# Hybrid decoder step on one core: the Gx tiles' tanh one tile later in the order, their first tap on ScalarE, past rows summed once, a sample's query fetched one turn ahead

## The reference

```
token_mixer(xn):
    z = xn @ w_in                      # one projection for all branches and gates
    qkv, _ = causal_dwconv(concat([g_q, g_k, g_v]), hist['gdn_conv'], w)   # width 4, 1536 channels
    q, k, v = split(silu(qkv)); q = l2norm(q); k = l2norm(k)
    o_b = gated delta rule over (q, k, v), in chunks; rmsnorm; times silu(g_z)
    ya, _ = causal_dwconv(a_c * a_h, hist['sconv'], w)                     # width 3, 512 channels
    yc, _ = causal_dwconv(c_v * sigmoid(c_g), hist['conf'], w)             # width 31, 512 channels
    o_d = forgetting attention; for a sample: over 2048 past tokens, 16 cached pages of 128
    x += (sum_i sigmoid(gate_i) * (o_i @ w_branch[i])) @ w_out
cross attention; then
    g, u = xn @ w_ffn_in;  x += (silu(causal_dwconv(g, hist['ffn'], w)) * u) @ w_ffn_out   # width 3, 2816 channels
```

## Time and profile before

| | us |
|---|---|
| median of 3 runs | 1837.2 |
| lowest, highest | 1836.98, 1845.5 |
| the profiled execution | 1836.28 |
| its span | 1834.5 |
| TensorE busy in it | 1545.2 (84%) |
| VectorE busy | 917.6 (50%) |
| GpSimd busy | 643.9 (35%) |
| ScalarE busy | 555.8 (30%) |

### The profile page before, as it was taken

How to read it: one execution, slowest core, us unless ns; L and a number is a source line. 1 busy time by engine, 2 the same in 40 slices (tenths; PEclk the granted TensorE clock), 3 DMA queues, 4 the chain that set the end, 5 groups by cost and what they waited for, 6 DMA issues and landing times. The chain is left out here.

```text
span 1834.5 us, 28395 instructions
## 1 busy us (share of the span) xinstructions
PE 1545.2 (84%) x11127; PEld 1426.6 (78%) x11127; DVE 917.6 (50%) x1353; ACT 555.8 (30%) x893; POOL 643.9 (35%) x354
## 2 busy tenths in 40 slices
PE   4996577789796978999888879889577999999996
PEld 3896577579796977877666659888476999999995
DVE  4169887998956743113222232264425566663122
ACT  3322441112214212254222223444214333333222
POOL 1266544555664712222111104310402344443440
PEclk8898787899898989999889879999867999999998
DMA  7145323433353416447433106432312233332331
GB/s 213 48 132 155 110 81 98 134 103 114 110 149 104 129 51 199 143 146 227 119 110 116 41 13 195 131 92 81 121 46 75 81 93 93 93 93 77 96 99 47
DMA packets 250997, 199.86 MB, mean 109 GB/s; under 512 B 11620, under 2 KB 208797, under 8 KB 250456
## 3 DMA queue, kind: packets, MB, share of 16 engines
q1 hardware_dynamic: 234149, 169.47, 31.7%
q10 hardware_dynamic: 15723, 23.86, 3.8%
q0 software_dynamic: 992, 4.72, 0.7%
HBM read 187.89 MB, written 10.81 MB: 108 GB/s over the span
## 5 line engine op out<-in xcount | busy, mean ns | idle before, releaser
L762 POOL TENSOR_TENSOR rawl<-raw,wh 128x1024 fp32r<-128x1024 f32 (+2 forms) x196 | 428.6, 2188 | 1040.4 <-ACT wh L1145 1038.8
L802 PE MATMUL pb<-xh,wh 128*128 128x260 f32 x2176 | 649.9, 299 | 48.7 <-DVE xl L1516 22.6
L802 PE MATMUL pb<-xl,wh 128*128 128x260 f32 x2176 | 633.7, 291 | 0.0
L802 PE MATMUL pb<-xh,rawl 128*128 128x260 f32 x2176 | 632.0, 290 | 0.0
L802 PEld LDWEIGHTS pb<-xh,wh 128*128 128x128 f32 x2176 | 430.7, 198 | 65.9 <-issue 39.2
L802 PEld LDWEIGHTS pb<-xl,wh 128*128 128x128 f32 x2176 | 430.5, 198 | 0.7
L802 PEld LDWEIGHTS pb<-xh,rawl 128*128 128x128 f32 x2176 | 429.9, 198 | 0.0
L1145 ACT ACTIVATE wh<-raw 128x1024 fp32r<-128x1024 f32 (+2 forms) x208 | 201.6, 969 | 551.1 <-PE pb L802 521.7
L802 PE MATMUL sd<-ar 128*128 128x128 f32 (+5 forms) x1584 | 280.9, 372 | 96.2 <-DVE ar L1516 37.2
L802 PEld LDWEIGHTS sd<-ar 128*128 128x128 f32 (+4 forms) x1584 | 200.2, 199 | 142.0 <-issue 80.8
L773 POOL TENSOR_TENSOR ar<-ar 128x512 f32<-128x512 f32 x128 | 187.5, 1465 | 86.3 <-DMA ar<-in_cache_fox_k 58.5
(11 more groups left out here) (168 smaller groups left out, 1739.6 us busy)
## 6 DMA issues: line engine op xcount, KB each, us to landing
raw<-in_w_in SPq DMA_DIRECT2D x80, 512.0 KB, 4.1
ar<-in_cache_fox_k SPq DMA_DIRECT2D x128, 256.0 KB, 2.7
ar<-in_cache_fox_v SPq DMA_DIRECT2D x128, 256.0 KB, 3.1
raw<-in_w_ffn_in SPq DMA_DIRECT2D x44, 512.0 KB, 3.7
raw<-in_w_branch SPq DMA_DIRECT2D x32, 256.0 KB, 3.2
raw<-in_w_ffn_out SPq DMA_DIRECT2D x16, 512.0 KB, 3.9
ar<-in_cache_mem_k ACTq DMA_DIRECT2D x1, 4096.0 KB, 19.5
raw<-in_w_out SPq DMA_DIRECT2D x8, 512.0 KB, 3.9
```

What stands on the lines that cost most here:

```text
L762: pool.tensor_tensor(rawl[:, p % RING, 0:kt, :], raw[:, p % RING, 0:kt, :], wh[:, p % (AHEAD + 1), 0:kt, :].bitcast(F32), SUB).then_inc(lo ...
L802: return pe.matmul(o, l, r, start=start, stop=stop, skip_group_check=True)
```

## The change

- In `timeline()`, `evac`: for a Gx tile behind a Gx tile the second step (`evac2`) of the tile before is emitted behind the first step of this one; the last Gx tile's own follows at once. The `l2` steps wait one piece more.
- In `timeline()`, `background`: a flag `turned`; where a page that is the first of a sample (not the very first) is due and the flag is down, the flag is raised and nothing is emitted in that call.
- GpSimd asks for a sample's query behind the last product of the sample before, and waits for it at the sample's first product.
- ScalarE writes the last tap's product of Gx and `fg` tiles straight from PSUM, between the copy of the last columns and that of the tile; VectorE's product goes. `ah` tiles keep theirs.
- The past rows of all tiles are multiplied by their weights and summed once, in the prologue (`pasts`, seven VectorE instructions); a tile adds the sum in one small instruction. The waits between the taps in `conv` change accordingly.

```diff
--- before.py
+++ after.py
@@ -164,7 +164,7 @@
 
 SIDE = ([("AFTER", "fq", 0)] + [("sm", n) for n in range(4)]
         + [("AFTER", "fq")] + [("fqr", n) for n in range(2)] + [("KSTART",)]
-        + [x for n in range(4) for x in (("AFTER", "gx", 2 * n + 1), ("l2", n))] + [("l2", 4)]
+        + [x for n in range(4) for x in (("AFTER", "gx", min(11, 2 * n + 2)), ("l2", n))] + [("l2", 4)]
         + [("AFTER", "gx")]
         + [("gs", n) for n in range(9)]
         + [("gdn", n, c) for c in range(2) for n in range(-1, 18)]
@@ -215,11 +215,16 @@
 def timeline():
 
     out, pos, step_n, tile, at_piece, bg = [], [0], [0], [0], [-1], {"tap": None, "k": None, "v": None}
+    turned = [False]
     size = {"tap": N_TAP, "k": N_PAGE, "v": len(V_EVENTS)}
 
     def background(kind, n):
         for _ in range(n):
             if bg[kind] is not None and bg[kind] < size[kind]:
+                if kind == "k" and bg[kind] % PAGES == 0 and bg[kind] > 0 and not turned[0] and n < 10:
+                    turned[0] = True
+                    return
+                turned[0] = False
                 out.append(V_EVENTS[bg[kind]] if kind == "v" else (kind, bg[kind]))
                 bg[kind] += 1
 
@@ -253,8 +258,12 @@
     def evac(upto_piece):
 
         while tile[0] < len(MT_LAST) and MT_LAST[tile[0]] <= upto_piece:
-            out.append(("evac", tile[0]))
-            out.append(("evac2", tile[0]))
+            m = tile[0]
+            out.append(("evac", m))
+            if MT_KIND[m] == "gx" and MT_KIND[m - 1] == "gx":
+                out.append(("evac2", m - 1))
+            if MT_KIND[m] != "gx" or MT_KIND[m + 1] != "gx":
+                out.append(("evac2", m))
             tile[0] += 1
 
     def through(mark):
@@ -634,6 +643,10 @@
             "ef": [(tail_ff, 4 * j, min(4, KF - 4 * j), 10, 2, out["ff_p"][0, 0, :, 512 * j:min(512 * (j + 1), FF)],
                     out["ff_s"][:, 0, FCW - 2, 512 * j:min(512 * (j + 1), FF)]) for j in range(6)]}
 
+        gh = cols[:, B_GS:B_GS + 4, 0:72].rearrange("p n (b r) -> p n b r", b=2)
+        sh = cols[:, B_SS, 0:64].rearrange("p (b r) -> p b r", b=NB)
+        fh = cols[:, B_FS:B_FS + 4, 0:88].rearrange("p n (b r) -> p n b r", b=2)
+
         def both(x):
 
             return x.rearrange("p (a b) -> p a b", a=2)
@@ -762,15 +775,21 @@
                 pool.tensor_tensor(rawl[:, p % RING, 0:kt, :], raw[:, p % RING, 0:kt, :],
                                    wh[:, p % (AHEAD + 1), 0:kt, :].bitcast(F32), SUB).then_inc(lo.sem, 1)
 
+            def query(b):
+
+                pool.dma_start(qb[:, :], qscr[b:b + 1, :].to_broadcast([P, 512])).then_inc(qb_in, 16)
+
             def product(i):
 
+                if i == 0:
+                    pool.wait_ge(qs_out, 16)
+                    query(0)
                 if i % PAGES == 0:
-                    if i == 0:
-                        pool.wait_ge(qs_out, 16)
-                    pool.dma_start(qb[:, :], qscr[i // PAGES:i // PAGES + 1, :].to_broadcast([P, 512])).then_inc(qb_in, 16)
                     pool.wait_ge(qb_in, 16 * (i // PAGES + 1))
                 pool.wait_ge(page_in[i % 4], 16 * (i // 4 + 1))
                 own(pool.tensor_tensor(kring[:, i % 4, :], kring[:, i % 4, :], qb[:, :], MUL), prod_done)
+                if i % PAGES == PAGES - 1 and i < N_PAGE - 1:
+                    query(i // PAGES + 1)
 
             for p in range(AHEAD):
                 split(p)
@@ -1190,6 +1209,9 @@
                     n_ = 11 if kind == "gx" else 10
                     act_c.by(act.activation((tail_gx if kind == "gx" else tail_ff)[:, idx, :],
                                             pb[:, m % 2, 1, TH - n_:TH], ACT.Copy))
+                    y, w = (gx_tile(idx), col(V_GW + 36 + idx)) if kind == "gx" else \
+                        (pairA[:, s, :], cols[:, B_FW, 2 * KF + idx:2 * KF + idx + 1])
+                    act_c.by(act.activation(both(y), x, ACT.Copy, scale=w))
                     fn(both(cb[:, s, 3:3 + T]), x, ACT.Copy, mt_act)
                 elif kind == "ac":
                     fn(both(pairA[:, s, :]), x, ACT.Copy, mt_act)
@@ -1527,20 +1549,22 @@
             def red(o, x, op, st=dve_c):
                 own(dve.tensor_reduce(o, x, AX, op), st)
 
-            def conv(x, y, width, wcol, hist, w_last, st):
-
-                ts(y, x[:, 3:3 + T], w_last)
+            def conv(x, y, width, wcol, past, st):
+
+                ys = y[:, SEQ:T] if len(past.shape) == 2 else y[:, SEQ:T].rearrange("p (n b) -> p n b", b=2)
                 for j in range(width - 1):
                     if j:
-                        dve.wait_ge(dve_c.sem, dve_c.n - 1)
-                    dve_c.by(dve.scalar_tensor_tensor(out=y[:, 0:SEQ], in0=x[:, 4 - width + j:4 - width + j + SEQ],
-                                                      scalar=wcol(j), in1=y[:, 0:SEQ], op0=MUL, op1=ADD))
-                    past = hist(j)
-                    ys = y[:, SEQ:T] if len(past.shape) == 2 else y[:, SEQ:T].rearrange("p (n b) -> p n b", b=2)
-                    if j:
-                        dve.wait_ge(dve_c.sem, dve_c.n - 1)
+                        dve.wait_ge(dve_c.sem, dve_c.n - (j == 1))
                     (st if j == width - 2 else dve_c).by(dve.scalar_tensor_tensor(
-                        out=ys, in0=past, scalar=wcol(j), in1=ys, op0=MUL, op1=ADD))
+                        out=y[:, 0:SEQ], in0=x[:, 4 - width + j:4 - width + j + SEQ], scalar=wcol(j), in1=y[:, 0:SEQ], op0=MUL, op1=ADD))
+                    if j == 0:
+                        dve_c.by(dve.tensor_tensor(ys, ys, past, ADD))
+
+            def pasts(h, w, width, n):
+
+                tt(h, h, w, MUL)
+                for j in range(1, width - 1):
+                    tt(h[..., 0:n], h[..., 0:n], h[..., j * n:(j + 1) * n], ADD)
 
             def evac(m, second):
                 p = MT_LAST[m]
@@ -1570,17 +1594,12 @@
                     stt(glu[:, idx, CFW - 1:CFW - 1 + T], pairB[:, s, :], 1.0, pairA[:, s, :], ADD, MUL)
                     cp(tail_cf[:, idx, :], glu[:, idx, SEQ:SEQ + 38], ev_all)
                 elif kind == "gx":
-                    gh = cols[:, B_GS:B_GS + 4, 0:72].rearrange("p n (b r) -> p n b r", b=2)
-
-                    def hist(j):
-                        return gh[:, :, :, j * 12 + idx]
-
-                    conv(cb[:, s, :], gx_tile(idx), GCW, lambda j: col(V_GW + 12 * j + idx), hist, col(V_GW + 36 + idx), ev_y)
+                    conv(cb[:, s, :], gx_tile(idx), GCW, lambda j: col(V_GW + 12 * j + idx), gh[:, :, :, idx], ev_y)
                 elif kind == "ah":
                     tt(both(cb[:, s, 3:3 + T]), both(pairA[:, s, :]), x, MUL, mt_dve)
                     cp(tail_sc[:, idx, :], cb[:, s, SEQ + 1:SEQ + 11])
-                    conv(cb[:, s, :], pairB[:, s, :], SCW, lambda j: col(V_SW + 4 * j + idx),
-                         lambda j: cols[:, B_SS, 0:64].rearrange("p (b r) -> p b r", b=NB)[:, :, 4 * j + idx], col(V_SW + 8 + idx), ev_all)
+                    ts(pairB[:, s, :], cb[:, s, 3:3 + T], col(V_SW + 8 + idx))
+                    conv(cb[:, s, :], pairB[:, s, :], SCW, lambda j: col(V_SW + 4 * j + idx), sh[:, :, idx], ev_all)
                 elif kind == "ab":
                     tt(both(tmp), both(pairB[:, s, :]), x, MUL, mt_dve)
                 elif kind.startswith("br"):
@@ -1599,12 +1618,7 @@
                     stt(both(xT[:, idx, :]), x, 0.5 if kind == "wo" else 1.0, both(xT[:, idx, :]), MUL, ADD, mt_dve)
                     cp(fl8[:, 0:1], fl8[:, 1:2], ev_all)
                 elif kind == "fg":
-                    fh = cols[:, B_FS:B_FS + 4, 0:88].rearrange("p n (b r) -> p n b r", b=2)
-
-                    def hist(j):
-                        return fh[:, :, :, j * KF + idx]
-                    conv(cb[:, s, :], pairA[:, s, :], FCW, lambda j: cols[:, B_FW, KF * j + idx:KF * j + idx + 1], hist,
-                         cols[:, B_FW, 2 * KF + idx:2 * KF + idx + 1], ev_y)
+                    conv(cb[:, s, :], pairA[:, s, :], FCW, lambda j: cols[:, B_FW, KF * j + idx:KF * j + idx + 1], fh[:, :, :, idx], ev_y)
                 elif kind == "fu":
                     tt(both(tmp), both(pairA[:, s, :]), x, MUL, mt_dve)
 
@@ -1936,6 +1950,9 @@
             red(own_head, ident.rearrange("p (j r) -> p r j", r=32)[:, 0:FH, :], ADD)
             dve.wait_ge(wsm_hi.sem, 1)
             tt(wsl[:, :, :], wsm[:, :, :], wsh[:, :, :].bitcast(F32), SUB, wsm_lo)
+            for x, w, width, n in ((gh, cols[:, B_VEC, V_GW:V_GW + 36], GCW, 12), (fh, cols[:, B_FW, 0:44], FCW, KF)):
+                pasts(x, w[:, None, None, :].to_broadcast([P, 4, 2, (width - 1) * n]), width, n)
+            pasts(sh, spread(cols[:, B_VEC, V_SW:V_SW + 8], NB, 1), SCW, 4)
             spl = [0]
             for e in TIMELINE:
                 if e[0] == "nsq" and e[1] in ADDED and e[2] > 0:
```

## The result

The changed kernel takes 1898.4 us (median of 4 runs, 1896.55 to 1906.49), the kernel before 1839.1 beside it (4 runs): a ratio of 1.0316, 95% interval 1.0289 to 1.0343. The forecast was 1871 us, the range 1842 to 1908. The profiled execution took 1899.5 us, its span is 1897.7.

The account below looks back on a forecast made before the run. VectorE was taken to bound the stretch before 517 us, and TensorE the feed-forward stage. From 1836.3 us, +119 for pages emitted together at piece 61, -80 path relief and -4 for queries gave 1871 us, range 1842 to 1908.

Parts of the forecast that it names:

- The heap: At piece 61, 74 pages emitted at once, 1.40 us each plus four sample starts of 3.9: +119 us, ends 114 and 142.
- The relief on VectorE: Before piece 45 (517 us), page sums, stretching, first taps and past rows together take 104 us off VectorE.
- (a): Before 517 us, 75 page sums at 0.66 us leave VectorE: 50 us.
- (b): Before 517 us, VectorE's two-input instructions stretch less without GpSimd's page products beside them: 31 us, ends 0 and 55.
- the two signs named ahead: Tap times before piece 45: near 0.75 us would show the relief right, still over 1 us would show it wrong.
- (c): Before 517 us, the first tap of 12 Gx tiles goes to ScalarE: 13 us off VectorE.
- (d): Before 517 us, past rows need 12 small instructions instead of 36, and 4 of the A tiles instead of 8: 10 us.
- From VectorE to the path: Before 517 us, TensorE's 97 us idle less 17 for norm turns and chunk starts: path gain 80, ends 50 and 115.
- half the relief: Rival: splits, not products, do the stretching and delta-rule steps are bound by their own chain; gain 45, 1910 us; chance 0.10.
- The two queries: Queries behind pages 96 and 112 find their cover in the new order: 4 us gained, ends 0 and 7.
- TensorE runs without a gap: Rival: between pieces 12 and 45 chains close, all 115 us comes back, heap at 1.34 us a page; 1832 us; chance 0.11.
- The flag works as its words say: Rival: pages keep their pace, each sample one turn later, no heap; some 45 us gained, 1791 us; chance 0.05.

Follow-up runs that it names:

- flag alone: The kernel before plus only the changed kernel's `turned` flag, with old convolution, tanh order and query fetch: 1914.8 us, ratio 1.0388.
- short sums: The kernel before with VectorE's sums of pages 16 to 90 taken over 8 of a head's 64 elements: 1832.2 us, ratio 0.9942.
- short products: The kernel before with GpSimd's products of pages 16 to 90 over 64 of 512 columns, sums whole: 1811.5 us, ratio 0.9834.
- convolution alone: The kernel before with only `conv`, `pasts` and ScalarE's first tap from the change: 1835.0 us, ratio 0.9963.
- order alone: The kernel before with only the new order (a Gx tile's tanh behind the next tile's first step, norms one piece later): 1836.7 us, ratio 0.9965.
- products on VectorE: The changed kernel without the flag, with products of pages 16 to 90 moved from GpSimd to VectorE, ahead of their sums: 1838.0 us, ratio 0.9987.
- products wait, 12 to 44: The changed kernel without the flag; in pieces 12 to 44 GpSimd's page products wait for VectorE's chain work of the turn: 1832.4 us, ratio 0.9958.
- without the flag: The changed kernel with its four flag lines taken out, so pages keep the old pace: 1827.2 us, ratio 0.9919.
- mended flag: The changed kernel, but only a page lowers the flag, not a tap, so pages are held one turn per sample: 1840.5 us, ratio 0.9987.
- products wait, 12 to 23: The changed kernel without the flag; in pieces 12 to 23 GpSimd's page products wait for VectorE's chain work of the turn: 1825.1 us, ratio 0.9919.
- taps and pages moved behind: The changed kernel without the flag, with 10 pages and 8 taps moved behind piece 44: 1833.5 us, ratio 0.9965.
- fewer pages, late: The changed kernel without the flag, one page per two turns up to piece 44, 7 per four behind, samples' steps later: 1816.6 us, ratio 0.9846.

## Why the prediction was right, and where it was mis-sized

The forecast had the direction and both large terms, and 1898 lies in its range. It is still 27 us above the 1871, because its terms erred to the same side: some 19 of it are the relief, 3 the heap, 3 the queries, and 2 came behind piece 62.

**The order** was right as read from the code: no page from piece 13 to 44, 74 pages in one heap.

**The heap** was right in place and price: 119 forecast, 122.2 measured; 1.40 and 3.9 forecast, 1.43 and 4.2 measured, and nothing covers it.

**The relief on VectorE** was 94.0 us (340.98 to 246.98), forecast 104. The pages' part, (a) and (b), was right as a sum: 81 forecast, 79.7 with the flag alone. How it splits was not shown by it, and short sums and short products show that the two terms do not add like this: what leaves VectorE changes what the rest falls beside. The taps came out between the two signs named ahead: 970 ns, neither near 750 nor over 1000. Convolution and past rows, (c) and (d), together with the new order brought 14.3 (261.25 to 246.98) instead of 23. The 9 are here, in VectorE's groups of the changed kernel and in order of time:

```profile
L1662 DVE SCALAR_TENSOR_TENSOR ar<-xT,cols,ar 128x512 f32<-128x512 f32 x112 | 103.3, 970 | 1.2
L1558 DVE SCALAR_TENSOR_TENSOR ar<-ar,cols 128x512 f32<-128x512 f32 x44 | 42.4, 962 | 18.7 <-ACT ar L1164 18.2
...
204.37 1.70 DVE L1558 SCALAR_TENSOR_TENSOR ar<-ar,cols 128x512 f32<-128x512 f32 x1 [4.13 <-ACT ar L1164]
...
203.12 2.40 POOL L775 TENSOR_TENSOR rawl<-raw,wh 128x1024 fp32r<-128x1024 f32 x1 [12.02 <-ACT wh L1164]
```

The 44 convolution taps take 962 ns; with the old convolution and no pages, 747: 9.5 us. A row of that kernel, the one with the flag alone, shows one way there. VectorE's first tap stood beside the split and waited for it:

```profile
203.43 2.01 DVE L1524 TENSOR_SCALAR ar<-ar,cols 128x520 f32<-128x520 f32 x1 [2.06 <-ACT ar L1150]
...
202.77 2.39 POOL L767 TENSOR_TENSOR rawl<-raw,wh 128x1024 fp32r<-128x1024 f32 x1 [11.36 <-ACT wh L1150]
```

Of its 2.01 us some 0.5 are its own work (0.49 where GpSimd does nothing beside it). In the changed kernel this instruction is gone and the next one has the wait: 1.70 us, to 206.07, behind the split's end at 203.12 + 2.40 = 205.52. I had priced the first tap at its mean of 1.05 us with the wait in it. The Trainium skill ("SBUF — State Buffer", Who interferes with whom) has VectorE and GpSimd share a port pair as a lock that is held for a whole instruction; these rows agree.

The removal is not the only way there. These are the same 44 taps with convolution alone, then with the order alone, where the first tap is still VectorE's (938 ns before):

```profile
L1544 DVE SCALAR_TENSOR_TENSOR ar<-ar,cols 128x512 f32<-128x512 f32 x44 | 46.0, 1044 | 8.7 <-ACT ar L1150 8.0
...
L1540 DVE SCALAR_TENSOR_TENSOR ar<-ar,cols 128x512 f32<-128x512 f32 x44 | 45.0, 1022 | 0.6
```

Beside a split lie 7 and 10 of them, against 1 before and 10 in the changed kernel (counted in the traces). So the new order too moves splits beside the convolution, and how the 9 us divide between the two stays open.

**From VectorE to the path** is the step that failed in its size. It took 97 us of idle TensorE, left 17 of it standing, and made 80. Measured were 60.0 (381.8 to 321.8), and otherwise composed: TensorE's idle time fell from 97.1 to 49.2, not to 17; and its busy time fell from 284.7 to 272.6 for the same 1966 matmuls, as the mean granted clock rose from 0.84 to 0.88, which the sum had put at nothing and only the far end of the range at 18. That was luck: without these 12 the relief would have been 48, about the 45 of "half the relief". What is left idle, by TensorE's waits from 135 to 456.8 us (the 4.3 for GpSimd end at 134.5, ahead of the stretch, and are not in the 49.2). The last row is the largest of the kernel before, from 135.6 to 517.4:

```profile
PE sd L821 <- DVE ar L1734: 14.2, 3, 4.7
PE sd L821 <- ACT ar L1384: 10.0, 2, 6.3
PE pb L821 <- ACT ar L1164: 8.3, 2, 7.5
PE sd L821 <- DVE ar L1538: 6.1, 9, 2.5
PE sd L821 <- issue: 5.9, 1, 5.9
PE pb L821 <- POOL rawl L775: 4.3, 1, 4.3
PE sd L821 <- ACT ar L1357: 3.0, 1, 3.0
...
PE sd L802 <- DVE ar L1720: 27.7, 3, 10.4
```

The norm turns (L1734 and L1357) are 17.2 where I had 12. Three of the four waits end with VectorE's scaling (L1734), as they did before (L1720); my 4 us a turn had only ScalarE's steps. The chunk starts (L1384) are 10.0 where I had 5. The other 22 are waits that I had not listed: the start of piece 15, 7.5 us, which was there before too; the delta rule's hand-overs between VectorE and TensorE; the first step after the Gx pieces. They were all in the waits of before and I took them to close with VectorE's load. VectorE is busy 77% of the new stretch, so it is hardly the bound of every turn any more. Over all kernels here the two go together like this:

| kernel | VectorE busy, us | piece 12 to 45, us |
|---|---|---|
| products on VectorE | 349.2 | 382.1 |
| order alone | 348.2 | 377.9 |
| products wait, 12 to 44 | 341.1 | 377.8 |
| before | 341.0 | 381.8 |
| without the flag | 334.7 | 371.5 |
| mended flag | 332.6 | 371.6 |
| convolution alone | 330.7 | 378.7 |
| products wait, 12 to 23 | 325.9 | 365.8 |
| taps and pages moved behind | 321.9 | 367.2 |
| short sums | 318.5 | 372.0 |
| short products | 298.5 | 351.1 |
| fewer pages, late | 292.6 | 345.6 |
| flag alone | 261.3 | 333.2 |
| changed | 247.0 | 321.8 |

From before to the changed kernel it is 60.0 for 94.0, 0.64 us of length for one of work; I had used 0.77 (80 for 104). With the measured 60 in its place the sum is 1836.3 + 119 - 60 - 4 = 1891. That VectorE's total carries the large differences fits the table, and products on VectorE from piece 24 on; it is not shown apart, since the stretching is both a part of that total and an effect of the order. It is not all: order alone and convolution alone lie 17.5 us of work apart and only 0.8 of length, and short products lie 20.9 us below short sums for 20.0 of work. How much of a product's price is its place in the turn stays open.

**The smaller parts.** The two queries, -4: the waits are gone from pieces 45 to 61, but these pieces became only 0.8 us shorter. ScalarE's copies in the feed-forward stage were put at 0. Pieces 140 to 183 take 257.8 us against 255.3 before, which looks like a cost; but with the flag alone, where ScalarE has no such copies, they take 257.5, and with convolution alone, where it has them, 255.5. So these 2 us are not the copies'; what they are stays open.

**The table loads.** The forecast held no drain, and the changed kernel shows none: in ScalarE's order of time a norm's logarithm begins at the end of its table load (208.79 + 1.28 = 210.07).

```profile
208.79 1.28 ACT L1164 ACT_TABLE_LOAD   x1
210.08 1.13 ACT L1164 ACTIVATE ar<-sd,ar 128x1040 f32<-128x1040 f32 x1
```

**The rivals.** "Half the relief" had 45 and 1910; the relief is about midway between it and the forecast, the time nearer to it. "TensorE runs without a gap" is out, with 49 us idle. "The flag works as its words say" was priced at 1791; mended, it is 1840, so its rival was worth nothing as a version, and the 45 us in it were much the same error: waits of GpSimd and ScalarE (24 and 66 us) counted as time on the path, while the stretch with the mended flag became 10.2 us shorter.

## What to carry to other kernels

Idle time of the waiting engine is not what a relief gives back: list each of its waits with what releases it, and let only those close whose releaser gets faster; here half of 97 us closed. Work that a flag holds back must be looked for in the whole order, to the point that forces it out: 75 pages taken from a full stretch gained 49 us, and 74 of their kind cost 125 in a heap with nothing beside them. And what a long engine's work is worth is told by taking it away, not by its length: GpSimd's 24 us of query waits were nearly all still there in the version that gains, and its 117 us of products, moved to VectorE, gained in one stage and lost more in the next.

## What the hardware showed that I had not expected

A tiny instruction of VectorE can wait beside a split as long as a large one. This is VectorE and GpSimd in order of time, in the kernel whose products wait in pieces 12 to 23:

```profile
194.35 2.35 DVE L1571 TENSOR_TENSOR ar<-ar,cols 128x8 f32<-128x8 f32 x1
...
193.96 2.72 POOL L771 TENSOR_TENSOR rawl<-raw,wh 128x1024 fp32r<-128x1024 f32 x1
```

Eight columns, 0.16 us where no GpSimd instruction is beside them, took 2.35 beside a split, to the split's end. The page sums keep 0.67 to 0.69 in every kernel here that leaves them whole. In the kernel before the past rows' small instructions took 356 ns on the mean, with the flag alone 220: so a good part of what looks like their work is this wait, which need not leave with them.
